# Second group of rows: requested after the last key weights, statistics beside the first group's value units, norm and transposes behind them

## The reference, cut to what matters

```
mod = split(silu(c) @ w_ada + b_ada, 6)
h   = layer_norm(x) * (1 + mod[1]) + mod[0]
q, k, v, u, vb, ga, gb = split(h @ w_in)
q, k = axial_rope(q), axial_rope(k)
vn   = layer_norm(gelu(vb));  u = gelu(u)
```

## Time and profile before

| what | value |
|---|---|
| median of 3 runs | 973.14 us (973.07 to 973.97) |
| the profiled execution | 973.24 us |
| its span on the slowest core (core 0) | 971.6 us |
| spans of the eight cores | 965.4 to 971.6 us |
| TensorE busy | 890.9 us (92%) |
| VectorE, ScalarE, GpSimd busy | 476.4, 296.4, 238.9 us |

### The profile page before, as it was taken

The page is one execution under the profiler, slowest core; times in us unless marked ns, Lnnn a source line. Parts: engine busy times, 40 slices in busy tenths (PEclk is TensorE's granted clock), DMA queues, the critical chain, the costliest instruction groups (busy, mean ns, idle before and its releaser), DMA issues.

```text
span 971.6 us, 15211 instructions; the slowest of 8 cores (965.4 to 971.6 us)
## 1 busy us (share of the span) xinstructions
PE 890.9 (92%) x5273; PEld 426.7 (44%) x5273; DVE 476.4 (49%) x930; ACT 296.4 (31%) x408; POOL 238.9 (25%) x282
## 2 busy tenths in 40 slices
PE   0568998899899999999999999999999999999993
PEld 0324554444444444444444444444444444444442
DVE  2147675376642366567677422221111115777774
ACT  1215555499932223433433411111111111000000
POOL 5024442266532345545444022000000000000000
PEclk9999999999999999999999999999999999999997
DMA  8998976059730033236944159952220004323231
GB/s 172 173 200 206 179 170 98 2 119 167 150 112 0 1 99 108 66 109 147 190 109 109 44 90 161 160 87 44 44 36 9 1 1 152 122 96 130 87 109 45
DMA packets 57964, 99.68 MB, mean 103 GB/s; under 512 B 20896, under 2 KB 21408, under 8 KB 57888
## 3 DMA queue, kind: packets, MB, share of 16 engines
q0 software_dynamic: 21136, 40.44, 26.8%
q1 hardware_dynamic: 36752, 58.25, 19.6%
HBM read 118.14 MB, written 16.78 MB: 139 GB/s over the span
## 4 chain that ended last, share of the span: by engine, by line
PE 78%; DMA 8%; ACT 5%; DVE 3%; issue 3%; POOL 1%; another core or an unknown queue 0%; SPq 0%; DVEq 0%; ACTq 0%; POOLq 0%
PE bank L1078 31%; PE bank L953 17%; PE bank L1209 15%; DMA arena<-wada 6%; PE bank L984 5%; ACT arena L812 3%; PE bank L488 2%; DMA arena<-xh 2%; PE bank L809 1%; PE bank L558 1%; PE bank L805 1%; PE bank L828 1%; PE bank L528 1%; ACT arena L428 1%; PE bank L540 1%
## 5 line engine op out<-in xcount | busy, mean ns | idle before, releaser
L1078 PE MATMUL bank<-arena 128*128 128x512 bf16 x1408 | 304.9, 379 | 0.0
L1078 PEld LDWEIGHTS bank<-arena 128*128 128x128 bf16 x1408 | 137.8, 98 | 166.1 <-issue 0.4
L953 PE MATMUL bank<-arena 128*128 128x512 bf16 x768 | 167.7, 379 | 0.0
L1089 DVE TENSOR_TENSOR arena<-bank,arena 128x512 bf16<-128x512 f32 x88 | 60.6, 691 | 212.4 <-PE bank L1078 202.3
L1209 PE MATMUL bank<-arena 128*128 128x512 bf16 (+1 forms) x748 | 152.2, 366 | 0.0
L1087 ACT ACTIVATE arena<-bank 128x512 f32<-128x512 f32 x88 | 52.0, 594 | 209.3 <-PE bank L1078 208.6
L953 PEld LDWEIGHTS bank<-arena 128*128 128x128 bf16 x768 | 75.1, 98 | 90.4
L1209 PEld LDWEIGHTS bank<-arena 128*128 128x128 bf16 x748 | 73.2, 98 | 79.1
L969 DVE TENSOR_TENSOR arena<-bank,arena 128x512 f32<-128x512 f32 x64 | 43.3, 690 | 84.0 <-PE bank L953 65.5
L812 ACT ACTIVATE arena<-bank 128x1024 bf16<-128x1024 f32 x80 | 76.3, 1026 | 5.3 <-PE bank L809 5.1
L962 ACT ACTIVATE arena<-bank 128x512 f32<-128x512 f32 x64 | 36.7, 591 | 108.9 <-PE bank L953 108.9
(11 more groups left out here) (108 smaller groups left out, 876.0 us busy)
## 6 DMA issues: line engine op xcount, KB each, us to landing
arena<-xh SPq DMA_DIRECT2D x34, 512.0 KB, 6.0
arena<-wada POOLq DMA_DIRECT2D x12, 1024.0 KB, 16.6
arena<-wff POOLq DMA_DIRECT2D x11, 1024.0 KB, 11.0
xmid_d<-arena SPq DMA_DIRECT2D x16, 512.0 KB, 2.9
arena<-xmid_d SPq DMA_DIRECT2D x16, 512.0 KB, 3.7
out<-arena SPq DMA_DIRECT2D x32, 256.0 KB, 2.2
arena<-wff POOLq DMA_DIRECT2D x11, 512.0 KB, 21.5
arena<-wout SPq DMA_DIRECT2D x16, 256.0 KB, 6.7
```

The costliest lines, as they stand in the source:

```text
L953: t_mm = S.op('pe', lambda e, k=k, n=n, p=bk(bank), lhs=w[:, lo + k, :], rhs=src[:, k, tok]: e.matmul(p, lhsT=lhs, rhs=rhs, start=(k == 0) ...
L1078: rhs=h2T[:, k, tok]: e.matmul(p, lhsT=lhs, rhs=rhs, start=(k == 0), stop=(k == 7)),
L1089: fb_free[b0 + 1] = sg_free[s_] = t_act[(f, tg)] = S.op('dve', lambda e, f=f, p=bk(b0 + 1), sg=sgb[s_]: e.tensor_tensor(out=act[f][:, tok] ...
```

## The change

The four loads of group 1 wait for `t_wqk[4]`, the last key weights, where they waited for the last modulation block. (The wait is in `ln_norm`, so the loads of later groups carry it too; by then it has long been fulfilled.) In group 0's side work the statistics of group 1 move from units 5 to 8 (u3, q2, q3, q4) to units 10 to 12 (vb1, vb2, vb3), with `ln_rstd` behind vb3 instead of behind q4. The norm, the transposes and the modulation of group 1 move from units 9 to 12 to a place behind group 0's v unit.

```diff
@@ ln_norm
         if g + 1 < len(groups):
-            x_load(g + 1, i, t_wada0[3])
+            x_load(g + 1, i, t_wqk[4])
@@
-    s0 = {5: [(ln_stats, 1, 0)], 6: [(ln_stats, 1, 1)], 7: [(ln_stats, 1, 2)], 8: [(ln_stats, 1, 3), (ln_rstd, 1)],
-          9: [(ln_norm, 1, 0), (ln_norm, 1, 1)], 10: [(ln_norm, 1, 2), (ln_norm, 1, 3)],
-          11: [(ln_turn, 1, (0, 1, 2, 3), (6, 7)), (ln_turn, 1, (4, 5, 6, 7), (2, 3))],
-          12: [(ln_out, 1, (0, 1, 2, 3), (6, 7), t_mod), (ln_out, 1, (4, 5, 6, 7), (2, 3), t_mod), (p0_issue,)]}
+    s0 = {10: [(ln_stats, 1, 0)], 11: [(ln_stats, 1, 1)], 12: [(ln_stats, 1, 2), (ln_stats, 1, 3), (ln_rstd, 1), (p0_issue,)]}
@@
     do(group_seq(0), s0)
     v_unit(0, u_bank((4, 5)))
+    for i in range(4):
+        ln_norm(1, i)
+    for cs, bs in (((0, 1, 2, 3), (6, 7)), ((4, 5, 6, 7), (2, 3))):
+        ln_turn(1, cs, bs)
+        ln_out(1, cs, bs, t_mod)
     rope_load(2)
```

## The result

The changed kernel takes 983.2 us where the kernel before takes 973.6: ratio 1.0101 (95% interval 1.0083 to 1.0119), 10 us slower. Run again on another occasion it was 1.0111 (1.0095 to 1.0127). Forecast were 983.4 us. (Medians in this part leave out executions in which the cores of one die ran at a lower granted clock than the others.)

What follows compares the result with a forecast made beforehand. TensorE, with 78% of the chain of waits, was taken as the bound. Earlier loads (-4.3 us) and the longer way from vb0 past group 1's q0 (+14.6) gave +10.3, so 983.4 us; range 977.8 to 987.8.

Steps and rivals of the forecast that it cites:

- Part 1: Group 1's tile loads held behind the key weights: `wvvb` lands sooner, so vb0 starts 4.3 us earlier (bounds 0.2 to 6.6).
- The delay in front: On idle q1, the tiles' first packets move 4 us after SyncE issues them; until then `wvvb` loads alone.
- the gain from being 0.2: Lower bound for vb0's earlier start: tiles share with `wvvb` at once, without issue delay, so only 0.2 us is gained.
- the 1.3 us: Time from a load's last bytes to its reported landing, used for the key weights and `wvvb`.
- First rival: Tiles and `wvvb` share at once, so the weights come no earlier: +14.4 us, 987.5; chance 0.10.
- Parts 2 and 3: Statistics behind the value units, norm and transposes behind the v unit: vb0 to the unit after q0 takes 14.6 us longer.
- vb0's norm: Step on VectorE after vb0's statistics and q4's rotation, beside GpSimd's rotation sum: 1.56 us.
- the ladder: Steps after vb0's start: last aggregate at 18.1 us, norms done 24.8, transposes 27.0, q0 starts 28.7, ends 32.2 at half clock.
- The queues: Moved steps delay no other work on GpSimd, SyncE, ScalarE or VectorE: the block's issue and group 2's tiles cost nothing.
- the 2 us named for that case: Price, some 2 us, if group 2's tiles, forecast for about 94 us, should come late after all.
- Rivals 2 and 3: Second: later TensorE waits absorb delay, 978.2, chance 0.07. Third: statistics add nothing to the chain, 968.8, chance 0.04.
- rival 3's condition: On VectorE, the last aggregate comes by about 9.6 us after vb0's start instead of 18.1; chance 0.04.

Runs made afterwards that it cites:

- e6_warm: The changed kernel with 50 unused matmuls added on TensorE in the gap between group 0's v unit and group 1's q0; 982.9 us, ratio 1.0092.
- e8_warm_to_q0: e6_warm with 10 further unused matmuls between the transposes and group 1's q0; 981.4 us, ratio 1.0083.

## Why the prediction was right

The direction and the size were right, and the size somewhat by luck: two terms were each 1.1 to 1.4 us too large, with opposite signs.

**Part 1, forecast -4.3 us.** Measured: -2.9 at vb0 on average over the cores, -3.2 by the undone load wait. On four of the eight cores vb0 starts later than the 64 to 66.5 that were named. The key weights landed on average when they should: SyncE issues the tiles behind that landing at 54.0 to 56.9, 55.4 on average, forecast 55.2. Core 7 is the last of them:

```profile
56.90 2.99 SPq L289 DMA_DIRECT2D arena<-xh  x4
```

The delay in front was as forecast: on this core q1 moved no packet from 52 to 60 us and six from 60 to 61, the first 3.8 us behind the issue (3.7 to 4.0 on the eight cores). Then the two queues shared, 51 and 45 packets from 61 to 62. Of the turn-taking that the Trainium skill describes ("DMA: Bandwidth & Descriptors", section "Queues, rings and completion order"): the trace agrees once both queues move, and the delay in front, which kept the gain from being 0.2, is not in that rule.

The mis-sized term is the end of `wvvb`. The sum lets its bytes end at the shared rate, at 63.9, and adds 1.3 us for the report. On core 7 all but 0.03 MB were moved at 64, but the last packets went only between 66 and 68 (DMA queue of the casting loads, 66 to 68 us):

```profile
q0 software_dynamic: 3, 0.00, 2.2%
```

The report came at 67.65, 0.13 us ahead of vb0. Of its 16 parts twelve were in at 63.5; over the cores the twelfth came at 64.1 and the last at 66.7 on average, in the kernel before at 68.5 and 69.6. So the 1.3 us are not a delay of the report (before, on core 0, the last packet ended at 69.13 and the report came at 69.47). They were the rest of a sum over bytes, taken from a load that ended alone; beside the tiles the last parts of a load trail by 2.6 us instead of 1.1. First rival refuted: vb0 did come earlier, and its 987.5 is what the kernel takes with the early loads (987.0).

**Parts 2 and 3, forecast +14.6 us from vb0 to the unit behind q0.** Measured 30.24 - 17.65 = 12.6 on the slowest core of each, and 13.5 as a mean of all cores: before, two of the eight ran vb0 at full clock (the key unit ahead of it had run at half, 3.2 us), which the row of one core did not show. The mis-sized term is vb0's norm, 1.56 us in the sum; here it took 0.46 (73.99 to 74.45). Both times it met GpSimd's rotation sum: on all eight cores of the kernel before it began 0.09 us ahead of the sum and took 1.65 us, on all eight of the changed kernel 0.14 us ahead and took 0.55, and the sum 1.53 instead of 1.27. What decides which of the two is held up no run shows. With 0.3 us less up to vb0's statistics and 0.2 less in each later norm the last aggregate ends at T + 16.3 instead of T + 18.1. The rest of the ladder is as forecast: first norm 2.0 behind it, four norms 4.63, transposes at half clock 2.3, modulation 1.45, q0 3.2.

**The queues.** The block's issue came no later (85.66) and was not waited for. Group 2's first tile was forecast for 94 and came at 98.3, 3.6 us after VectorE asked; TensorE did not wait for it, so the 2 us named for that case were not due.

**Rivals 2 and 3.** The delay is 10.6 us at 97 and 11.2 at 204 us, so nothing took it up. The statistics did not run in VectorE's idle time in front of vb0's own; that was rival 3's condition. On core 7 the four tiles landed at 65.7, 67.9, 69.2 and 70.5 and VectorE was idle until 71.8, so the loads left room for three of them; the order of emission kept the condition from being met.

## What to carry over

A piece of work that is moved behind other work on the same engine is priced by the chain that hangs on it and not by its own length: 6 us of statistics became 7.4 us of idle TensorE, and 4.6 us of norms became 6.1. Before moving work to make room for a transfer, look for the idle time that it fills now: here ScalarE stood idle for 7 us ahead of vb0's gelu, and filling that with the norms made the kernel 2 to 3 us faster, where moving statistics and norms further back made it 10 us slower. When a load on a second queue is held back, ask whether the transfer that should profit still ends beside it; held back one step further, the same loads gained some 4 us more (3.7 us at the unit behind q0, 4.1 by the ratios).

## Of the hardware, not expected

The last 2% of a 1.31 MB load took nearly 4 us beside a load on the other queue (0.03 MB left at 64 us, landing reported at 67.65), though the two queues had shared evenly before (51 and 45 packets from 61 to 62 us). TensorE's clock fell to half at q0 on six of eight cores, on one of them in the middle of it, after only 2.13 us of idle (e6_warm), though matmuls and transposes had kept it up from 78 us on; with ten matmuls in that wait it stayed up on all eight cores (e8_warm_to_q0). In the kernel before core 2's vb0 ran at full clock behind 1.94 us of idle, but there the clock had been at half in the key unit in front, from 64 to 67 us, and had come back. How much idle time is one too many is not settled by these runs.
